# Overwriting scatters with pre-summed doubles, and a different split of the last tokens' dots, in a PEER layer

## The reference, cut to what matters

```python
q = (t @ w_query).reshape(n_tok, P_HEADS, 2, P_DQ)
sc = jnp.einsum('thcd,hckd->thck', q, sub_keys)
s1, i1 = lax.top_k(sc[:, :, 0], P_TOPK)
s2, i2 = lax.top_k(sc[:, :, 1], P_TOPK)
cand = (s1[..., :, None] + s2[..., None, :]).reshape(n_tok, P_HEADS, P_TOPK * P_TOPK)
top_s, top_i = lax.top_k(cand, P_TOPK)
e1 = jnp.take_along_axis(i1, top_i // P_TOPK, axis=-1)
e2 = jnp.take_along_axis(i2, top_i % P_TOPK, axis=-1)
experts = e1 * P_NKEYS + e2
gates = jax.nn.softmax(top_s, axis=-1)
# for each token: y = sum over its 128 experts of gelu(t . u[e]) * gate * v[e]
```

## Time and profile before

| | |
|---|---|
| median of 3 runs | 5357.61 us (5350.65 to 5358.99) |
| profiled execution | 5357.13 us, span 5355.4 us |
| TensorE, matmul busy | 4472.7 us, 84% |
| VectorE busy | 3146.1 us, 59% |
| ScalarE busy | 1936.2 us, 36% |
| GpSimd busy | 1117.1 us, 21% |
| 384 scatters into the gate matrix, GpSimd | 656.1 us, mean 1709 ns |
| 128 u gathers, GpSimd | 154.8 us, mean 1209 ns |
| 128 v gathers, GpSimd | 214.1 us, mean 1673 ns |
| PEER phase, first scores to last v matmul | 3767 to 5333 us |

### The profile page before, as it was taken

How to read it: one execution, slowest core, us unless ns; L and a number is a source line. 1 busy time by engine, 2 the same in 40 slices (tenths; PEclk the granted TensorE clock), 3 DMA queues, 4 the chain that set the end, 5 groups by cost and what they waited for, 6 DMA issues and landing times. The chain is left out here.

```text
span 5355.4 us, 62778 instructions
## 1 busy us (share of the span) xinstructions
PE 4472.7 (84%) x23192; PEld 3793.6 (71%) x23192; DVE 3146.1 (59%) x4430; ACT 1936.2 (36%) x2287; POOL 1117.1 (21%) x811
## 2 busy tenths in 40 slices
PE   8936799999999749999799996777994157779999
PEld 3923478777787538878599995633994157779998
DVE  0062388889888652223488866612894034458887
ACT  0001267677676501111355545510432012223333
POOL 1000100000000000000000002000487888865432
PEclk9557899999999869999799995578997579889999
DMA  8412499999999733334211006133564367789997
GB/s 350 145 43 91 184 357 368 365 372 364 366 368 366 274 141 110 109 120 145 93 34 37 25 11 255 49 124 122 137 147 77 46 170 224 220 297 397 347 347 254
DMA packets 338405, 1077.74 MB, mean 201 GB/s; under 512 B 88372, under 2 KB 141188, under 8 KB 285540
## 3 DMA queue, kind: packets, MB, share of 16 engines
q1 hardware_dynamic: 232516, 865.03, 44.5%
q0 software_dynamic: 105696, 210.12, 13.4%
HBM read 917.31 MB, written 157.70 MB: 201 GB/s over the span
## 5 line engine op out<-in xcount | busy, mean ns | idle before, releaser
L3015 POOL DMA_INDIRECT gate_matrix<-peer_gate,peer_cell x384 | 656.1, 1709 | 205.8 <-issue 125.4
L84 PE MATMUL peer_bank<-peer_t_high,peer_high 128*128 128x384 f32 (+1 forms) x1152 | 421.7, 366 | 328.1 <-DVE peer_low L2794 328.0
L1076 DVE TENSOR_TENSOR moe_low<-moe_raw,moe_high 128x2048 fp32r<-128x2048 f32 x256 | 574.5, 2286 | 55.9 <-ACT moe_high L984 53.0
L84 PEld LDWEIGHTS peer_bank<-peer_t_high,peer_high 128*128 128x128 f32 x1152 | 232.1, 201 | 352.9 <-DVE peer_low L2794 347.7
L984 ACT ACTIVATE moe_high<-moe_raw 128x2048 fp32r<-128x2048 f32 x256 | 477.9, 1904 | 3.7 <-PE moe_up_bank L894 2.1
L2895 DVE SCALAR_TENSOR_TENSOR peer_ring<-peer_ring,peer_tok 128x1024 f32<-128x1024 f32 x128 | 156.6, 1225 | 479.0 <-DMA peer_ring<-expert_u_rows,peer_expert 478.8
L3102 ACT ACTIVATE peer_high<-peer_raw 128x1024 fp32r<-128x1024 f32 x272 | 287.2, 1056 | 346.3 <-PE peer_bank L86 276.5
L85 PE MATMUL peer_bank<-peer_t_low,peer_high 128*128 128x384 f32 (+1 forms) x1152 | 412.1, 358 | 0.0
L86 PE MATMUL peer_bank<-peer_t_high,peer_low 128*128 128x384 f32 (+1 forms) x1152 | 411.5, 357 | 0.0
L84 PE MATMUL peer_bank<-peer_hidden_high,peer_high 128*128 128x384 f32 x1024 | 344.7, 337 | 16.5 <-DVE peer_hidden_low L2889 16.5
L2794 DVE TENSOR_TENSOR peer_low<-peer_raw,peer_high 128x1024 fp32r<-128x1024 f32 x272 | 331.0, 1218 | 23.8 <-ACT peer_high L3102 23.7
(11 more groups left out here) (554 smaller groups left out, 10631.0 us busy)
## 6 DMA issues: line engine op xcount, KB each, us to landing
moe_raw<-w_gate_up SPq DMA_DIRECT2D x256, 1024.0 KB, 6.9
moe_raw<-w_down SPq DMA_DIRECT2D x128, 1024.0 KB, 7.4
peer_raw<-expert_u SPq DMA_DIRECT2D x128, 512.0 KB, 3.6
peer_raw<-expert_v SPq DMA_DIRECT2D x128, 512.0 KB, 7.2
rows<-mix_zero POOLq DMA_DIRECT2D x12, 2048.0 KB, 39.3
mix_ada_w<-w_ada SPq DMA_DIRECT2D x48, 512.0 KB, 3.6
zin_only_w<-w_in SPq DMA_DIRECT2D x48, 512.0 KB, 3.8
gate_matrix<-gla_zeros POOLq DMA_DIRECT2D x32, 768.0 KB, 32.3
```

Of the source, the lines that this page charges most:

```text
L84: pe.matmul(out, wh, xh, start=start, stop=False)
L1076: v.tensor_tensor(low[:, slot], raw[:, slot], high[:, slot].bitcast(F32), ALU.subtract).then_inc(gu_low, 1)
L3015: pool.indirect_dma_start(out=cells, out_offset=at_cell, in_=gate[:, t, h * TOPK + k:h * TOPK + k + 1], in_offset=None, compute_op=ALU.add ...
```

## The change

Four things. (1) The scatters lose `compute_op=ALU.add` and overwrite. For heads 1 to 7 they write `whole_gate` in place of `gate`: the gate of this head plus the gates of all earlier heads with the same expert. (2) VectorE makes that sum after the gates of each head from 1 on: for each of three token groups a comparison, a product and a reduction, each over 16 x 16h elements, chained, then one addition. (3) The heads take 8 u tiles each in place of 6 (`U1 = 8`, `PER = 10`), so that 80 tiles lie in the heads and 64 later; `low(10h + 13)` and `low(10h + 14)` stand in the summing of the doubles, and `exps(h)` stands behind `take(10h + 10)` and `cut(10h + 13)`. (4) 80 early dots in place of 112 (`EARLY = 5 * 16`), their gathers spread over the 144 scatters of heads 5 to 7, 5 for every 9; the other 48 dots stand beside the v tiles, one with every second tile, up to v tile 94. `weigh` and the gelus of heads 5 to 7 follow them.

```diff
-    U1 = 6
-    LATER, VBASE, LAST = 8 * HEADS, 8 * HEADS + 80, 8 * HEADS + 80 + PEER_KEYS
+    U1, PER = 8, 10
+    LATER, VBASE, LAST = PER * HEADS, 2 * HEADS + PEER_KEYS, 2 * HEADS + 2 * PEER_KEYS
-    RING, EARLY = 6, 7 * TOPK
+    RING, EARLY = 6, 5 * TOPK
...
+        D2 = Marks(s.sem("dve_doubles"), [f"{n}{t}" for t in range(TD) for n in ("same", "their", "sum")] + ["whole"])
...
-        place_u = lambda j: j if j < EARLY else EARLY + 2 * (j - EARLY) + 1
-        place_v = lambda j: EARLY + 2 * j if j < TOPK else EARLY + TOPK + j
+        place_v = lambda j: EARLY + j + min((j + 1) // 2, HEADS * TOPK - EARLY)
+        place_u = lambda j: j if j < EARLY else place_v(2 * (j - EARLY)) + 1
...
+        dotted = lambda h: 2 * ((h + 1) * TOPK - 1 - EARLY)
...
-                low(h * 8 + 12)
+                low(h * PER + 12)
+                if h:
+                    V.after(v, "gates", h)
+                    past = [P, TOPK, h * TOPK]
+                    same = whole[:, 12:16].rearrange("p a t -> p (a t)")[:, 0:h * TOPK * TOPK].rearrange("p (k j) -> p k j", k=TOPK)
+                    for t in range(TD):
+                        D2.mark(f"same{t}", h - 1, v.tensor_tensor(same, pair[:, t, 0:h * TOPK].unsqueeze(1).to_broadcast(past),
+                                                                   pair[:, t, head(h)].unsqueeze(2).to_broadcast(past), ALU.is_equal))
+                        D2.after(v, f"same{t}", h - 1)
+                        D2.mark(f"their{t}", h - 1, v.tensor_tensor(same, same, gate[:, t, 0:h * TOPK].unsqueeze(1).to_broadcast(past), ALU.mult))
+                        D2.after(v, f"their{t}", h - 1)
+                        D2.mark(f"sum{t}", h - 1, v.tensor_reduce(again[:, t], same, AX.X, ALU.add))
+                        D2.after(v, f"sum{t}", h - 1)
+                        if t < 2:
+                            low(h * PER + 13 + t)
+                    D2.mark("whole", h - 1, v.tensor_tensor(whole_gate[:, :, head(h)], again[:, 0:TD], gate[:, 0:TD, head(h)], ALU.add))
+                else:
+                    low(h * PER + 13)
+                    low(h * PER + 14)
...
-                if m == TOPK + 4:
-                    weigh(7)
+                for h in range(EARLY // TOPK, HEADS):
+                    if m == dotted(h) + 5:
+                        weigh(h)
                 row(m)
-                if m < TOPK:
-                    dot(EARLY + m)
+                if m % 2 == 0 and EARLY + m // 2 < HEADS * TOPK:
+                    dot(EARLY + m // 2)
...
             def scatter(h, k, t):
+                source = whole_gate if h else gate
                 at_cell = bass.IndirectOffsetOnAxis(ap=cell[:, t, h * TOPK + k:h * TOPK + k + 1], axis=0)
-                pool.indirect_dma_start(out=cells, out_offset=at_cell, in_=gate[:, t, h * TOPK + k:h * TOPK + k + 1], in_offset=None,
-                                        compute_op=ALU.add).then_inc(scattered, 16)
+                pool.indirect_dma_start(out=cells, out_offset=at_cell, in_=source[:, t, h * TOPK + k:h * TOPK + k + 1],
+                                        in_offset=None).then_inc(scattered, 16)
...
                 V.after(pool, "gates", h)
+                D2.after(pool, "whole", h - 1)
                 need(pool, scattered, 16 * TOPK * TD * h)
                 for k in range(TOPK):
                     for t in range(TD):
                         scatter(h, k, t)
-                    if h == 4 and k < RING:
-                        gather(u_rows, k, place_u(k))
+
                     if h > 4:
-                        for n in range(2):
-                            j = RING + (h - 5) * 2 * TOPK + 2 * k + n
+                        done = (h - 5) * TOPK + k
+                        for j in range(done * EARLY // (3 * TOPK), (done + 1) * EARLY // (3 * TOPK)):
                             gather(u_rows, j, place_u(j))
-            for j in range(RING + 6 * TOPK, EARLY):
-                gather(u_rows, j, place_u(j))
-            for j in range(TOPK):
+            for j in range(HEADS * TOPK):
                 gather(v_rows, j, place_v(j))
-                gather(u_rows, EARLY + j, place_u(EARLY + j))
-            for j in range(TOPK, HEADS * TOPK):
-                gather(v_rows, j, place_v(j))
+                if j % 2 == 0 and EARLY + j // 2 < HEADS * TOPK:
+                    gather(u_rows, EARLY + j // 2, place_u(EARLY + j // 2))
...
-                if k % 8 == 0 and 0 < k <= LATER:
-                    exps(k // 8 - 1)
+                if k % PER == 0 and 0 < k <= LATER:
+                    exps(k // PER - 1)
```

More of the change, by code:

```diff
@@ L2774, in peer_phase @@
                   + ["negmax", "pos0", "pos1", "posf", "topf"] + [f"{n}{c}" for c in range(2) for n in ("is", "at", "e")]
-                  + ["pair", "cell", "expert", "inv", "gates"])
+                  + ["pair", "inv", "cell", "expert", "gates"])
+        D2 = Marks(s.sem("dve_doubles"), [f"{n}{t}" for t in range(TD) for n in ("same", "their", "sum")] + ["whole"])
         A = Marks(s.sem("act_steps"), n1("exp"))
@@ L2865, in _ @@
                     V.mark(f"e{c}", h, v.tensor_reduce(key[:], four, AX.X, ALU.add))
-                    low(h * 8 + 10 + c)
+                    low(h * PER + 10 + c)
                 V.after(v, "e1", h)
-                V.mark("pair", h, v.scalar_tensor_tensor(pair[:], key2[:], float(PEER_KEYS), key1[:], ALU.mult, ALU.add))
-                V.after(v, "pair", h)
-                V.mark("cell", h, v.scalar_tensor_tensor(cell[:, :, head(h)], pair[:, 0:TD], float(DENSE),
-                                                         token[:, 0:TD].unsqueeze(2).to_broadcast([P, TD, TOPK]), ALU.mult, ALU.add))
-                V.mark("expert", h, v.tensor_copy(expert[:, head(h)], pair[:, TD]))
+                V.mark("pair", h, v.scalar_tensor_tensor(pair[:, :, head(h)], key2[:], float(PEER_KEYS), key1[:], ALU.mult, ALU.add))
                 A.after(v, f"exp{TT - 1}", h)
@@ L2876, in _ @@
                 V.after(v, "inv", h)
+                V.mark("cell", h, v.scalar_tensor_tensor(cell[:, :, head(h)], pair[:, 0:TD, head(h)], float(DENSE),
+                                                         token[:, 0:TD].unsqueeze(2).to_broadcast([P, TD, TOPK]), ALU.mult, ALU.add))
+                V.mark("expert", h, v.tensor_copy(expert[:, head(h)], pair[:, TD, head(h)]))
                 V.mark("gates", h, v.tensor_tensor(gate[:, :, head(h)], eg[:], esum[:].unsqueeze(2).to_broadcast([P, TT, TOPK]), ALU.mult))
-                low(h * 8 + 12)
+                low(h * PER + 12)
[17 more added lines that the diff above has]
+                    low(h * PER + 14)
             def gating(m):
@@ L2915, in _ @@
                     dot(j)
-                for h in range(7):
+                for h in range(EARLY // TOPK):
                     if due(k - 5) >= (h + 1) * TOPK > due(k - 6):
```

42 lines of the change are left out of this document (22 added, 20 removed).

## The result

The changed kernel takes **5104.6 us** (median of 4 runs, 5102.8 to 5109.3) against 5356.4 for the kernel before (5350.7 to 5359.0): a ratio of 0.9533, 95% interval 0.9516 to 0.9549. The forecast was 5113. The profiled execution has a span of 5101.8 us.

The account below looks back on a forecast made before the run. GpSimd's queue of scatters and gathers, from 3805.6 us on, was taken to set when v begins: 4535 (v's start) + 554 (v) + 22.2 (tail) + 1.7 = 5113 us, range 5050 to 5240.

Parts of the forecast that it names:

- Step 1, the price x: GpSimd's queue: each scatter without the add or u gather costs 1.47 us, 0.20 of it lost to VectorE; bounds 1.37, 1.62.
- Step 2, VectorE in the heads: Heads: summing doubled experts' gates adds 81 us to VectorE over seven heads; the heads end at 4200.
- The new wait at `inv`: Heads: VectorE stands 4.4 us in each head at the reciprocal, since the exps now come behind a later tile.
- Step 3, GpSimd's queue: Heads and later u: 72.8 us of scatters a head, head 5 starts at 4170, the last scatter goes out at 4506.
- Step 4, into v: From last scatter to first v matmul: landing of 2.2 us plus 26.6; v begins at 4535, against 4789.5 before.
- Step 5, v: v with 48 dots beside its tiles takes 410 + 133 + 11 = 554 us, transfers at 408 GB/s.
- v is held by transfers at 361 GB/s: Rival in v: 167 MB take 463 us at that rate, v 607, the kernel 5166 us; chance 0.13.
- the add is not what the 1.55 us paid for: Rival on scatters: 4-byte elements cost it, so only the moved gathers gain, v at 4750, 5324 us; chance 0.07.
- VectorE holds GpSimd off at half a step or fully: Rival in heads and later u: x 1.75, 5236 us, chance 0.09; or x 2.49, 5580 us, chance 0.02.
- GpSimd off the path: Rival: TensorE ends later u at 4445, v begins at 4455, the kernel takes 5033 us; chance 0.05.

Follow-up runs that it names:

- e2: The changed kernel with the add put back into its scatters, which write each head's own gate: 5324.4 us, one run.
- e10: The changed kernel with a 0.54 us GpSimd fill behind each scatter of heads 0 to 4: 5205.8 us, ratio 0.9723.
- e12: The changed kernel with a 128 x 256 fill (some 0.3 us) behind each scatter of heads 0 to 4: 5155.4 us, ratio 0.9623.
- e11: The changed kernel with the last 16 early u gathers after the last scatter and eight gelu buffers instead of two: 5298.9 us, ratio 0.9902.
- c1: The changed kernel run again, unchanged, on another chip (B): 5291.9 us, ratio 0.9871.

## Why the prediction was right

The mechanism held: GpSimd's queue, priced by instruction, set the time. That the number did, took two pieces of luck. Two misses of opposite sign, v begun 6.3 us late and v 15.6 us shorter, left 9. And in the runs of the result the writes did not pile up: on chip B the same kernel takes 5291.9 us, outside the stated range of 5050 to 5240, and no rival had that case.

**Step 1, the price x.** Right. The two groups of scatters have means of 1.128 and 1.178 us, with the pause of 0.30 that is 1.43 and 1.48, against 1.47. The 0.20 us of it that were put down to VectorE are seen one by one. Timelines of GpSimd and of VectorE in the changed kernel, head 7's sums:

```profile
4183.23 1.00 POOL L3044 DMA_INDIRECT peer_ring<-expert_u_rows,peer_expert  x1 [0.30 <-issue]
4184.54 1.45 POOL L3039 DMA_INDIRECT gate_matrix<-peer_whole_gate,peer_cell  x1 [0.31 <-issue]
4186.30 1.61 POOL L3039 DMA_INDIRECT gate_matrix<-peer_whole_gate,peer_cell  x1 [0.30 <-issue]
4188.21 1.75 POOL L3039 DMA_INDIRECT gate_matrix<-peer_whole_gate,peer_cell  x1 [0.30 <-issue]
4190.27 0.98 POOL L3044 DMA_INDIRECT peer_ring<-expert_u_rows,peer_expert  x1 [0.30 <-issue]
```
```profile
4183.91 1.22 DVE L2798 TENSOR_TENSOR peer_low<-peer_raw,peer_high 128x1024 fp32r<-128x1024 f32 x1
4185.05 2.02 DVE L2888 TENSOR_TENSOR peer_shared<-peer_pair 128x1792 f32<-128x1792 f32 x1
4187.10 2.02 DVE L2891 TENSOR_TENSOR peer_shared<-peer_shared,peer_gate 128x1792 f32<-128x1792 f32 x1
4189.16 2.02 DVE L2893 TENSOR_REDUCE peer_again<-peer_shared 128x16 f32<-128x1792 f32 x1
```

The scatter at 4186.30 starts 0.77 us before the comparison ends (4187.07) and takes 0.64 us more than 0.97; that at 4188.21 starts 0.91 before the product's end and takes 0.78 more. The gather at 4190.27 starts under the reduction, with one input, and takes 0.98. So in these rows a maker of descriptors that starts under an operation with two inputs in SBUF waits about until that operation is over, and not under a reduction. Counted over the whole trace, 125 of the 384 scatters start with more than 0.15 us of such an operation still to run, 0.71 us on average, and take 0.61 us more than the median; none of the other 259 takes over 0.05 us more. The Trainium skill, SBUF — State Buffer, section "Who interferes with whom", infers that `tensor_tensor` doesn't stall GpSimd's DMAs, and says that with two inputs in SBUF it contends with GpSimd's reads; the rows above contradict the inference for the indirect ones.

**Step 2, VectorE in the heads.** Right in kind. The 63 operations of the sums took 25.7 + 25.7 + 25.6 = 77 us (forecast 81 with the additions). The new wait at `inv` is there with 4.9 us a head, forecast 4.4. Some 0.2 us of the difference come from a part of the change that its description leaves out: `cell` and `expert`, which stood ahead of `inv` (0.2 us in the trace before, 3956.63 to 3956.83), now stand behind it. The eight `inv` run from 3806.8 to 4183.4, 53.8 us apart on average, against the 55.2 of the forecast's periods. All that lies beside GpSimd's queue: in the profile of the result the first scatters of heads 1 to 4 come 1.9 us after the engine was free, as a landing takes, and those of heads 5 to 7 no later than 2.6, so none waits for `whole`.

**Step 3, GpSimd's queue.** Right. Head 5 starts at 4179.4 instead of 4170: 2.1 us come from a later first scatter, the other 7 from heads of 74.3 us instead of 72.8. From there to the last scatter it took 4515.4 - 4179.4 = 336.0 us, and the forecast had 4506 - 4170 = 336.

**Step 4, into v.** 25.9 us from the last scatter to the first v matmul, forecast 29: the gate rows' load starts at 4517.7, 2.3 us after the scatter, and v comes 23.6 after that, not 26.6.

**Step 5, v.** The one term that was mis-sized: 538.4 us instead of 554. From 4605 to 4955 the DMA engines moved 405 to 410 GB/s in every slice of 50 us, as assumed, and TensorE was busy all of each. In the window from 4555 to 4955 it did 2286 / 24 = 95.3 tiles, 4.20 us each, at 408 x 400 = 163 MB or 1.71 MB a tile: volume and rate were right. But the forecast added to them the 11 us that v had taken over 128 x 4.16 before. In the changed kernel v took 5.9 us over it in all: of the assumed sum of 11 for the transfers and 11 for the start, some 6 were there. The Trainium skill, DMA: Bandwidth & Descriptors, section "Where 436 GB/s comes from", puts HBM's side at about 358 GB/s for a core, as half of what it gives for a memory stack that two cores share; here one core worked alone, and its 408 GB/s over 400 us are above that share. The rival that v is held by transfers at 361 GB/s falls with the 408 GB/s and the 4.20 us a tile.

The differences add up: +2.1 + 7.2 (head 5) - 3.1 (into v) - 15.6 (v) = -9.4, and the span is 5101.8 instead of 5113 - 1.7 = 5111.3.

**Its sums.** Some recorded ones are off by a few microseconds. By their own terms (v's start + 554 + 22.2 + 1.7) the upper bound is 5180 and not 5190, and the rivals that have v at 4662, 4750 and 5005 end at 5240, 5328 and 5583, 3 to 4 us above what stands there. The last of the eight periods should be 58.2 + 4.4 = 62.6 and not 61.3. Nothing in the forecast hangs on them.

**The rivals.** That the add is not what the 1.55 us paid for is refuted by e2. That VectorE holds GpSimd off at half a step or fully is refuted by the mean of 1.18 us. GpSimd off the path is refuted by e2, e10 and e12 against the changed kernel: the last scatter goes out 219.7, 100.3 and 51.4 us later, and the kernels take 219.8, 101.2 and 50.8 us more.

**What it did not see.** No rival had the case that plain 4-byte writes at the new pace hold up the core's other transfers. The prediction took the duration of an instruction on GpSimd for its whole price, and the landing for the 2.2 us of before. The row for the plain scatter came from a stretch of 14 instructions with rows of 4 KB and so couldn't show it. On chip B it costs 187 us (5291.9 against 5104.6), three quarters of the gain. **Open** stays why none of the runs of the result was held up at the same pace. It is not known whether that chip differs from A, B and C: in the experiments every kernel with plain scatters at full pace met hold-ups, but each chip ran only some of the kernels. Where the writes wait on their way to memory no record shows, nor why some heads on one chip are spared. It also stays open whether 72 writes per us (e12) would be slow enough on chips A to C.

## What to carry to other kernels

Where one engine's queue of issued DMAs sets the time, price its instructions one by one, with what the other engines do to them, and follow only that queue to the end; here the sum held to 10 us in 5100 on a chip where nothing piled up. But an issue that gets cheaper also makes its transfers come denser: put bytes or writes per microsecond beside the duration, and compare them with what the trace has shown to flow. A change that rests on the densest pace should run on several chips, since one chip's time may hide or show a pile-up; a short filler behind each issue is a cheap test of it, and on chip C it was a cheap guard (5206 us against e11's 5299).

## What the runs showed of the hardware

- An indirect scatter of 128 elements that adds takes 1.55 us on GpSimd, a plain one 0.97, each with 0.30 us behind it. The add kept its own pace: 60 writes per us in e2.
- A scatter of the changed kernel that starts under a VectorE operation with two SBUF inputs takes 0.61 us more on average (125 of 384), one that doesn't takes 0.96 to 1.02 us.
- Plain scatters of 4 bytes at up to 100 writes per us stopped the core's tile transfers for 30 us and more at a time (0 GB/s, 3840 to 3870 in c1), in two to four of the first five heads, in runs on three chips; the profile of the result shows none of it at 83 per us. The tile transfers came back when the last scatter had been issued, the landing came some 40 us later. Held-up heads of c1 came through at 59 to 62 writes per us. A rate of 63 (e10) flowed on one of the three chips, 60 with the add (e2) on another.
- The same number of writes into 16 neighbouring rows instead of 16,384 was slower still (5378 us).
- In the stops TensorE had the lower clock: granted 0.50, that is 1.2 GHz, from 3830 to 3880 in c1, where it did 4 to 11 matmuls in 10 us, against 1.00 with 65 matmuls in 3810 to 3820, and 0.98 with 58 again in 3880 to 3890.
